# Hybrid encoder step on one core: paired state tables, slabs spread over pairs, and tile 0 decoded head by head

## The reference

```python
bu = einsum('gph,blgh->blgp', b_bar, u)            # 64 groups x 64 complex states, 16 inputs
h[t] = a_bar * h[t-1] + bu[t]                      # associative scan over positions
y = einsum('ghp,blgp->blgh', c, h).real + d * u    # then GELU and a gated unit
...
s = einsum('thcd,hcnd->thcn', q, keys)             # 8 heads, 2 halves, 128 keys
v1, i1 = top_k(s[:, :, 0], 16); v2, i2 = top_k(s[:, :, 1], 16)
cand = v1[..., :, None] + v2[..., None, :]         # 256 candidates
top_s, pos = top_k(cand, 16)
idx = i1[pos // 16] * 128 + i2[pos % 16]           # 8 x 16 = 128 experts for each token
g = softmax(top_s)
a = einsum('td,tkd->tk', x, u_tab[idx])            # one 2048-wide row for each token and expert
y = einsum('tk,tkd->td', gelu(a) * g, v_tab[idx])
```

## Time and profile before

| what | us |
|---|---|
| median of 3 runs | 4193.71 (4190.0 to 4196.06) |
| profiled execution | 4181.71 |
| its span | 4179.8 |
| VectorE busy | 2805.5 (67%) |
| TensorE busy | 2642.1 (63%) |
| GpSimd busy | 1239.6 (30%) |
| ScalarE busy | 345.2 (8%) |

### The profile page before, as it was taken

How to read it: one execution, slowest core, us unless ns; L and a number is a source line. 1 busy time by engine, 2 the same in 40 slices (tenths; PEclk the granted TensorE clock), 3 DMA queues, 4 the chain that set the end, 5 groups by cost and what they waited for, 6 DMA issues and landing times.

```text
span 4179.8 us, 31056 instructions
## 1 busy us (share of the span) xinstructions
PE 2642.1 (63%) x11464; PEld 2042.3 (49%) x11464; DVE 2805.5 (67%) x3300; ACT 345.2 (8%) x808; POOL 1239.6 (30%) x1386
## 2 busy tenths in 40 slices
PE   7989989989668677892988499970999500000000
PEld 6868577845454344551557477860887400000000
DVE  4350211389873888778779886298066598999998
ACT  0110221000001212101010000000000001000000
POOL 2440000012231222222222222023022256777772
PEclk9975579989559555895999799985999855555555
DMA  8653144488996899997999799698699998999997
GB/s 239 223 176 86 58 153 165 149 262 314 353 408 236 311 351 354 373 422 289 422 422 398 313 422 412 230 401 336 209 391 423 400 393 300 409 410 410 408 409 331
DMA packets 291063, 1334.30 MB, mean 319 GB/s; under 512 B 69536, under 2 KB 129472, under 8 KB 139488
## 3 DMA queue, kind: packets, MB, share of 16 engines
q0 software_dynamic: 140432, 952.56, 57.2%
q1 hardware_dynamic: 110384, 365.54, 23.9%
q10 hardware_dynamic: 40096, 14.22, 1.7%
HBM read 1284.43 MB, written 57.20 MB: 321 GB/s over the span
## 4 chain that ended last, share of the span: by engine, by line
DMA 34%; DVE 25%; PE 25%; issue 8%; POOL 6%; ACT 1%; ACTq 1%; SPq 0%; DVEq 0%; POOLq 0%
DMA arena<-in_peer_v,arena 20%; PE low L1418 10%; DVE arena L1238 7%; DVE acc L1251 7%; DMA expert_scratch<-arena 6%; PE low L1728 4%; POOL arena L572 3%; DMA arena<-c_scratch 3%; POOL arena L563 3%; PE low L1522 2%; DMA arena<-in_w 2%; PE low L1506 1%; PE acc L1481 1%; DVE low L1251 1%; DMA arena<-in_peer_u,arena 1%
## 5 line engine op out<-in xcount | busy, mean ns | idle before, releaser
L1251 DVE SCALAR_TENSOR_TENSOR acc<-arena,acc 128x2048 f32<-128x2048 f32 x443 | 1042.8, 2354 | 269.0 <-DMA arena<-in_peer_v,arena 247.3
L1418 PE MATMUL low<-arena 128*128 128x192 f32 (+1 forms) x4096 | 1036.9, 416 | 56.6 <-DMA arena<-in_w 36.0
L1728 PE MATMUL low<-arena 128*128 128x256 f32 x4096 | 906.0, 383 | 232.6 <-ACT arena L800 178.1
L1728 PEld LDWEIGHTS low<-arena 128*128 128x128 f32 x4096 | 779.2, 191 | 359.3 <-issue 193.1
L1418 PEld LDWEIGHTS low<-arena 128*128 128x128 f32 x4096 | 742.2, 195 | 342.3 <-issue 33.6
L563 POOL DMA_INDIRECT arena<-in_peer_v,arena x576 | 558.5, 970 | 1061.8 <-DVE acc L1251 790.5
L1238 DVE SCALAR_TENSOR_TENSOR arena<-arena,acc 128x2048 f32<-128x2048 f32 x320 | 724.3, 2284 | 79.1 <-DMA arena<-in_peer_u,arena 72.7
L563 POOL DMA_INDIRECT arena<-in_peer_u,arena x320 | 320.9, 1003 | 1464.8 <-DVE arena L1238 981.5
L1251 DVE SCALAR_TENSOR_TENSOR low<-arena,low 128x2048 f32<-128x2048 f32 x126 | 296.5, 2353 | 18.4 <-DMA arena<-in_peer_v,arena 15.4
L572 POOL DMA_INDIRECT arena<-expert_scratch,arena x256 | 248.0, 969 | 77.9 <-issue 77.9
L1196 DVE TENSOR_REDUCE arena<-arena 128x8 f32<-128x128 f32 x5 | 1.4, 284 | 236.8 <-ACT arena L780 236.8
(11 more groups left out here) (265 smaller groups left out, 2044.7 us busy)
## 6 DMA issues: line engine op xcount, KB each, us to landing
arena<-in_w SPq DMA_DIRECT2D x128, 1024.0 KB, 6.2
arena<-in_ut SPq DMA_DIRECT2D x128, 1024.0 KB, 17.7
expert_scratch<-arena SPq DMA_DIRECT2D x128, 128.0 KB, 15.0
arena<-bias_scratch SPq DMA_DIRECT2D x16, 640.0 KB, 5.6
arena<-in_peer_v,arena POOLq DMA_INDIRECT x576, 12.2
arena<-toeplitz_scratch SPq DMA_DIRECT2D x64, 128.0 KB, 4.8
arena<-c_scratch SPq DMA_DIRECT2D x64, 128.0 KB, 5.4
bias_scratch<-distance_scratch POOLq DMA_DIRECT2D x1, 5120.0 KB, 25.7
```

What stands on the lines that cost most here:

```text
L1251: stt(held, slot[j], wv_, held, ALU.mult, ALU.add).then_inc(used, 1)
L1418: ins = mm(L[n % 2][:, 0:width], wring[n % 2][:, k, :], rhs(k), start=k == 0, stop=k == KT - 1)
L1728: ins = mm(L[j % 4][:, 0:NSD], ud[j % 4][:, k, :], lane(catB, k)[:, P:NB], start=k == 0, stop=k == KT - 1)
```

## The change

Five edits:

1. Both parts of a table (real and imaginary) are made by one instruction on twice the width, with negated copies of B and of the powers (`NBi`, `NWr`) so that both parts are a sum: three instructions in place of six on VectorE (256 elements) and on GpSimd (288). The first two no longer wait for each other.
2. The 24 slabs are spread over the 32 pairs: three pairs with a slab, then one without. Before, pairs 0 to 23 had one.
3. `place` of tile 0 comes before its first head.
4. Tile 0 is decoded behind each head (`decode_head`, 32x16 elements), each signals `idx_ready`, and GpSimd may gather that head's 16 rows. Slots 2 and 3 of the ring, which lie on tile 0's scores, open from row 16 on.
5. Behind each of heads 1 to 7 VectorE takes two rows. The calls after that are as before, `rows_to(72)` and `rows_to(96)` among them.

```diff
-SLOT_FROM = [0, 0, 0, 0, STEPS[0] + 6, R_U2 + 16]
+SLOT_FROM = [0, 0, TOPK, TOPK, STEPS[0] + 6, R_U2 + 16]
...
             for g in range(GP):
-                if g < 24:
-                    weights(N_QA + g, 1)
+                if g % 4 < 3:
+                    weights(N_QA + 3 * (g // 4) + g % 4, 1)
...
-                for r, (w1, c1, w2, c2) in enumerate(((Wr, Cr, NWi, Ci), (NWi, Cr, Wr, Ci))):
-                    link(nc.gpsimd.tensor_tensor(tP[0], wv(w1), cvv(c1), ALU.mult))
-                    link(nc.gpsimd.tensor_tensor(tP[1], wv(w2), cvv(c2), ALU.mult))
-                    link(nc.gpsimd.tensor_tensor(CAz[g % 4][:, r, :].rearrange("p (k h) -> p k h", k=NW), tP[0], tP[1],
-                                                 ALU.add if r == 0 else ALU.subtract))
+                nc.gpsimd.tensor_tensor(tP[0], wv(WrNWi), cvv(Cr), ALU.mult)
+                link(nc.gpsimd.tensor_tensor(tP[1], wv(NWiNWr), cvv(Ci), ALU.mult))
+                link(nc.gpsimd.tensor_tensor(CAz[g % 4].rearrange("p r (k h) -> p r k h", k=NW), tP[0], tP[1], ALU.add))
...
             def gather(i):
-                if s == 0 and kind == "u" or i == R_V3 or i == R_V4:
-                    pool.wait_ge(idx_ready, t + 1)
+                if i < KK:
+                    if s % TOPK == 0:
+                        pool.wait_ge(idx_ready, s // TOPK + 1)
+                elif s == 0 and kind == "u" or i == R_V3 or i == R_V4:
+                    pool.wait_ge(idx_ready, PH + t)
...
                 elif j < 4:
                     pool.wait_ge(placed, 1)
                     pool.wait_ge(x1_stored, 32)
+                    if j >= 2:
+                        pool.wait_ge(idx_ready, PH)
...
-                link(tt(tD[0], wv(Wr), bv(Br), ALU.mult))
-                link(tt(tD[1], wv(Wi), bv(Bi), ALU.mult))
-                link(tt(Gb[g % 2][:, 0], tD[0], tD[1], ALU.subtract))
-                link(tt(tD[0], wv(Wr), bv(Bi), ALU.mult))
-                link(tt(tD[1], wv(Wi), bv(Br), ALU.mult))
-                link(tt(Gb[g % 2][:, 1], tD[0], tD[1], ALU.add))
+                tt(tD[0], wv(Wr), bv(BrBi), ALU.mult)
+                link(tt(tD[1], wv(Wi), bv(NBiBr), ALU.mult))
+                link(tt(Gb[g % 2], tD[0], tD[1], ALU.add))
...
+            def decode_head(t, h):
+                pu = pos2.bitcast(U32)
+                tp = topp[:, TOPK * h:TOPK * h + TOPK]
+                nc.vector.tensor_scalar(pu[:, 0:TOPK], tp, 4, None, ALU.logical_shift_right)
+                link(nc.vector.tensor_scalar(pu[:, TOPK:2 * TOPK], tp, 15, None, ALU.bitwise_and))
+                link(nc.vector.tensor_copy(pos2[:, 0:2 * TOPK], pu[:, 0:2 * TOPK]))
...
+                link(tt(e4, pos2[:, 0:2 * TOPK].rearrange("p (c k) -> p c k", c=2).unsqueeze(3).to_broadcast(full),
+                        iota.unsqueeze(1).unsqueeze(1).to_broadcast(full), ALU.is_equal))
+                link(tt(e4, e4, i12[:, :, h, :].unsqueeze(2).to_broadcast(full), ALU.mult))
+                link(nc.vector.reduce_sum(row[0][:, 0:2 * TOPK], eq.rearrange("p (k j) -> p k j", j=TOPK), AX.X))
+                link(stt(idx[:, t * KK + TOPK * h:t * KK + TOPK * h + TOPK], row[0][:, 0:TOPK], float(NKEY),
+                         row[0][:, TOPK:2 * TOPK], ALU.mult, ALU.add))
                 dve.sem_inc(idx_ready, 1)
...
-            dve.wait_ge(score_out, 1)
+            dve.wait_ge(score_out, 2)
+            place(0, x1s[0])
             for h in range(PH):
                 head(0, h)
-                if h == 3:
-                    dve.wait_ge(score_out, 2)
-                    place(0, x1s[0])
-            decode(0, nothing)
+                decode_head(0, h)
+                if h:
+                    rows(2)
+            logits(0)
+            link.zero()
             for h in range(PH):
                 rows(2)
                 head(1, h)
...
             for g in range(GP):
-                if g < 24:
-                    slab(N_QA + g, xa, NA)
+                if g % 4 < 3:
+                    slab(N_QA + 3 * (g // 4) + g % 4, xa, NA)
                 if g + 1 < GP:
                     g_turn(g + 1)
```

More of the change, by code:

```diff
@@ L180, in build @@
         HsB = at(H3, 2 * GP * (CB + 1)).rearrange("p (r g c) -> p r g c", r=2, g=GP)
-        Br, Bi, Cr, Ci = (at(H6 + 512 * i, 512).rearrange("p (g h) -> p g h", g=GP) for i in range(4))
-        Wr, Wi, NWi = (at(H6 + 2048 + 288 * i, 288).rearrange("p (g k) -> p g k", g=GP) for i in range(3))
-        sm = [at(H6 + 2912 + 32 * i, 32) for i in range(30)]
+        NBi, Br, Bi, Cr, Ci = (at(H6 + 512 * i, 512).rearrange("p (g h) -> p g h", g=GP) for i in range(5))
+        BrBi, NBiBr = (at(H6 + o_, 1024).rearrange("p (r g h) -> p r g h", r=2, g=GP) for o_ in (512, 0))
+        Wr, NWi, NWr, Wi = (at(H6 + 2560 + 288 * i, 288).rearrange("p (g k) -> p g k", g=GP) for i in range(4))
+        WrNWi, NWiNWr = (at(H6 + 2560 + 288 * i, 576).rearrange("p (r g k) -> p r g k", r=2, g=GP) for i in range(2))
+        sm = [at(H4 + 32 * i, 32) for i in range(30)]
         (are, aim, ldt, h0r, h0i, dt, er, th, rn, cosv, sinv, nr, den, fr, fi, ta, tb) = sm[:17]
@@ L187, in build @@
         CAz = [at(FO + 512 + 288 * j, 288).rearrange("p (r n) -> p r n", r=2) for j in range(4)]
-        tD = [at(FO + 1664 + 128 * j, 128).rearrange("p (k h) -> p k h", k=SL) for j in range(2)]
-        tP = [at(FO + 1920 + 144 * j, 144).rearrange("p (k h) -> p k h", k=NW) for j in range(2)]
+        tD = [at(FO + 3744 + 256 * j, 256).rearrange("p (r k h) -> p r k h", r=2, k=SL) for j in range(2)]
+        tP = [at(FO + 4256 + 288 * j, 288).rearrange("p (r k h) -> p r k h", r=2, k=NW) for j in range(2)]
         GT = [at(FO + 2208 + 256 * j, 256) for j in range(4)]
@@ L487, in _ @@
                 products_out(j)
-            sp.wait_ge(idx_ready, NT)
+            sp.wait_ge(idx_ready, PH + NT - 1)
             sp.wait_ge(v_stored, 32)
@@ L520, in _ @@
             for g in range(GP):
-                wv = lambda t: t[:, g, :].unsqueeze(2).to_broadcast([P, NW, SG])
-                cvv = lambda t: t[:, g, :].unsqueeze(1).to_broadcast([P, NW, SG])
+                wv = lambda t: t[:, :, g, :].unsqueeze(3).to_broadcast([P, 2, NW, SG])
+                cvv = lambda t: t[:, g, :].unsqueeze(1).unsqueeze(1).to_broadcast([P, 2, NW, SG])
                 if g >= 4:
@@ L585, in _ @@
                     sum_store(1)
-            pool.wait_ge(idx_ready, NT)
+            pool.wait_ge(idx_ready, PH + NT - 1)
             for b in range(2):
@@ L651, in _ @@
             for g in range(GP):
-                if g < 24:
-                    n = N_QA + g
-                    dst = qA[:, g] if g < 8 else kT[:, g - 8, 0:NA] if g < 16 else vA[:, g - 16]
-                    out_of(n, dst, L[n % 2][:, 0:NA], DH ** -0.5 if g < 8 else None)
+                if g % 4 < 3:
+                    i = 3 * (g // 4) + g % 4
+                    dst = qA[:, i] if i < 8 else kT[:, i - 8, 0:NA] if i < 16 else vA[:, i - 16]
+                    out_of(N_QA + i, dst, L[(N_QA + i) % 2][:, 0:NA], DH ** -0.5 if i < 8 else None)
                 if g + 1 < GP:
@@ L972, in _ @@
             link(tt(Bi, tm[2], tm[3], ALU.add))
+            link(ts_(NBi, Bi, -1.0, None, ALU.mult))
             def times(dr, di, ar, ai, br, bi):
@@ L984, in _ @@
             link(ts_(NWi, Wi, -1.0, None, ALU.mult))
+            link(ts_(NWr, Wr, -1.0, None, ALU.mult))
             link(nc.vector.tensor_copy(HsA[:, 0, :, 0], h0r))
@@ L1186, in decode, with logits @@
                              tokoff[:, t - NGU:t - NGU + 1], ALU.mult, ALU.add))
+                logits(t)
+                dve.sem_inc(idx_ready, 1)
+                link.zero()
+            def logits(t):
                 tt(rowg[t].rearrange("p (h k) -> p h k", h=PH), topv, topv[:, :, 0:1].to_broadcast([P, PH, TOPK]),
```

8 lines of the change are left out of this document (6 added, 2 removed).

## The result

| | before | after |
|---|---|---|
| median, first comparison | 4193.31 us (4 runs, 4190.0 to 4196.06) | 4215.7 us (4 runs, 4211.1 to 4221.07) |
| median, second comparison | 4202.31 us (15 runs) | 4216.51 us (8 runs) |
| profiled execution, its span | 4181.71, 4179.8 us | 4211.5, 4209.5 us |

The change makes the kernel slower: ratio 1.0054 (95% interval 1.0037 to 1.0072), in the second comparison 1.0033 (1.0022 to 1.0043). That is +22 us, then +14 us; the prediction's sum was +16.5 us.

What follows compares the result with a forecast made beforehand. TensorE bounds the tables, VectorE their last eight pairs and tile 0; gathers and tables share DMA in the y products. Tile 0 +27.5 and tables -11 give +16.5 us on the median 4193.7: 4210, range 4197 to 4224.

Steps and rivals of the forecast that it cites:

- tile 0: Part 1, rows moved forward: carried state 42.5 us later, y stretch -11, y stores -4, together +27.5 us.
- the tables: Part 2, table stretch: -11 for the pairs, +3 clock, -4.7 end, +1.5 copies, together -11 us (-18 to +3).
- Start, decoding, first wait: VectorE in tile 0: later first copy +4.4 us, decoding by head +9.0, waits for gathered rows -1.9.
- 14 rows at 2.21: +31.0: VectorE ahead of the carried state: 14 rows moved forward at 2.21 us each add 31.0 us.
- Absolute times: Signs in the trace after: first y product at about 1110 us, tables ending near 265 us.
- y stretch: -11, a length of 153.7: y products: gathers end 39 us sooner, last pairs go at 3.2 us, so 153.7 against 164.5 us: -11 (-8 to -35).
- Stores: -4 (0 to -8): ScalarE's eight y stores: with gathers over, 13.6 us to issue in place of 17.13, -4 us.
- Clock: +3 (0 to +14): TensorE idling 1.9 us in each of seven slab-less pairs: clock falls at about 2 us each, taken as +3 us.
- the clock falls in every slab-less pair: Rival in the table stretch: seven falls of 2 us instead of +3, so +11 and 4221 us; chance 0.14.
- Stall beside the second input block: kept, 0 +/- 2: Table stretch, load of the second input block: TensorE's 4.60 us stall stays, 0 +/- 2 us.
- Build 2.1 us, end of the stretch: Tables: VectorE's build 2.1 us, a slab-less pair 3.0; stretch end behind slabs -4.7 us, copies meeting slab loads +1.5.
- The wider GpSimd operation: GpSimd's 288-wide table operation: length on no row, 0.43 to 0.86 us, middle value taken; skill estimate 0.75.

Runs made afterwards that it cites:

- the two halves: Edits 1 and 2 alone, and edits 3, 4 and 5 alone, each on the kernel before: ratios 0.9986 and 1.0043.
- Decode alone: Kernel before with edits 3, 4 and 5 but without the 14 rows between the heads: ratio 1.0017 (1.0007 to 1.0028).
- tables only: Kernel before with edits 1 and 2 alone, tile 0 as before: 4195.56 us, ratio 0.9986 (0.9974 to 0.9997).
- Tables filled: Edits 1 and 2 on the kernel before, TensorE repeating state products in the pair ahead of each slab-less one: 4192.6 us, ratio 0.9979.

## Why the prediction was right

The sum was +16.5 us. From the two traces of each kernel S + Y + W gives 563.7 - 542.6 = +21.1 and T, with the means above, -3.6: **+17.5**; the two halves measured alone give 18 - 6 = +12, the two comparisons +22 and +14. The forecast stands, but part of that is luck: tile 0 was put at +27.5 us and is +21.1, the tables at -11 and are about -4, and the two errors cancel.

- *Start, decoding, first wait.* The prediction had +4.4, +9.0 and -1.9. One head's decoding is 816.81 - 813.73 = 3.08 us for 3.05, the eighth ends 109.2 us behind the start for 109, the round of a head with two rows 14.5 us for 14.4. Rows 14 and 15 waited 3.6 us in place of the 7.5 of the first two before, so the wait term was -3.9 for -1.9. Decode alone says +7.4 for the terms without rows (+6.1).
- *14 rows at 2.21: +31.0.* Measured +31.3. The carried state came 41 us later for 42.5.
- *Absolute times.* The first y product was to start at about 1110 us and started at 1120.85: the -11 for the tables were in that number. T gave 3.4 of them in this trace, and the first state products came 6.1 us late, which the unchanged kernel does too. The tables were to end near 265 us and end at 282.13.
- *y stretch: -11, a length of 153.7.* Measured 151.6 and 154.3, mean 11.0 under that of before. The split (6 pairs fast, then 5.55 until the gathers end, then 3.2) was read off before and found in after, with 5.7 for 5.55. VectorE waits 36.0 and 39.1 us at row 96 in the two traces (near 50 was forecast), since the stores ahead of it got shorter too.
- *Stores: -4 (0 to -8).* ScalarE's issue fell from 17.13 to 10.12 us. Over all traces it is 14.6 to 19.0 us where gathers run beside it and 10.0 to 10.3 in the six where they are over; W is 98.9 to 104.4 and 93.0 to 93.8. The mechanism was right, the term too small by almost 4 us: W fell by 7.7, the far end of its bounds. The price had been taken from loads of the same size (13.6 us); the stores alone take 10.
- *Clock: +3 (0 to +14).* **This step failed.** I put 1.88 us of idling between rows of 1.60 and 2.12 us and took a value near the harmless one. All seven pairs lost the clock, at 1.9 us a round: 13 us. From the first to the last state products -11 + 3 = -8 us was forecast; the three traces with both edits have 188.2, 190.6 and 193.4 us against a mean of 191.3 in the seven without, so on average nothing was gained there. It was the rival "the clock falls in every slab-less pair", and its mechanism was there; its total of 4221 was not.
- *Stall beside the second input block: kept, 0 +/- 2.* Also wrong: it fell from 4.60 us, with a slow slab behind it (7.15 for 5.47), to 0.70 us; in the second trace to 2.10 with a slab of 7.11, with tables only to 2.30 with one of 5.47. Tables filled shows why: there TensorE has kept the clock for three rounds, comes sooner and waits 5.24 us. Wait and slow slab together, 2.5 to 5.6 us of the clock's price came back here, and filling the idle time gained little.
- *Build 2.1 us, end of the stretch.* The build (106.8 to 109.1) and the 3.2 us of a pair (3.0) were right. From the last state products to the y products of block A it is 91.54 + 215.6 - 282.13 = 25.0 instead of 28.9 us, -3.9 for -4.7 + 1.5, and 24.9 with tables only. But the second trace of after has 29.4 and no gain. There TensorE idled 2.91 instead of 1.44 us ahead of block B's two slabs, came back at a granted clock of 0.50 for 5.9 us, and took 23.84 instead of 20.88 us for them. The lower clock can be met there too, which the forecast left out; why that wait was longer is open.
- *The wider GpSimd operation.* The 0.87 us that 288 elements take on average in after (L528, 32 of them, 870 ns) are not its own length, for VectorE works beside it. Alone it is 0.68 us (at 46.73, 47.36), where 144 elements take 0.43, alone as well as beside VectorE: the middle value, 0.64, was near. The Trainium skill, GPSIMD Engine Reference, section 3.1, has 4497 ns for 2048 elements, from which the prediction's estimate was 0.75 us; the trace has 0.68 and, for the third operation of a table (at 48.12), 0.80. VectorE's second and third operation take 0.90 and 0.78 us beside it, the first, ahead of it, 0.42. The Trainium skill, SBUF — State Buffer, section "Who interferes with whom", has the two exclude each other for a whole instruction; the trace fits, since from 124.75 us on the two engines' operations end by turns: 125.17, 125.71, 125.99, 126.52, 126.80 and 127.45.

The tables part as a whole was put at -11 (-18 to +3) and is -4 to -6: within the range, at a third to a half of the size. The smaller cost of tile 0 (3.7 us at the stores, 2.7 at the carried state) made up for it.

## What to carry to other kernels

Work that is moved is priced at both ends: a row cost 2.2 us where VectorE set the time and nothing where it waited, and the same loop with fewer rows ahead of the carried state gained about what the change lost. Ask of each stretch whether its shared resource is full: taking work out of a full one gives time back only from the moment when that work is used up (14 rows fewer in the y stretch: 11 us, 26 fewer: 24). What more work would cost there, no run shows. Where a short idle time of TensorE is added between two measured cases, take the dear one, and look whether a later wait swallows it. And read the length of an operation where the other engine rests: beside VectorE GpSimd's 0.68 us looked like 0.87.

## What was not expected of the hardware

- The unchanged kernel's spans were 4179.8 and 4210.5 us in two profiled executions, and its 23 runs of one comparison spread from 4192.0 to 4211.3. GpSimd's issue of the same gathers had a mean of 955 or 1028 ns in the last 300 us. A difference of two single traces here says nothing below 30 us; stretches between fixed events repeat within 3 us in S and Y, 5 in W, and 5 in T (10 with spread slabs).
- TensorE lost its clock after 1.88 us of idling between slabs in all seven pairs of both traces of after (slab 6.2 to 7.7 us for 5.47) and in six of seven of tables only, and after 0.95 us in three of seven pairs of one execution and not in the other four.
- The y products of block B ran at a granted clock of 0.50 from end to end, in after and before, with the DMA engines at 411 to 412 GB/s in the stretch of slow pairs.
- GpSimd's 288-element operation takes 0.68 us alone and 0.85 to 0.92 beside VectorE's.
